# Expert rows turned by ScalarE and VectorE, hidden rows' transposes inside the gate/up product, and a second pair of PSUM banks for the down product

## The reference, cut to what matters

```python
h2 = rms_norm(x, norm2_g)
# each row picks the best of 4 groups, then 2 of the 8 experts in it (32 experts)
# its copies are sorted by expert and padded to blocks of 128 rows
def run_block(args):
    toks, e = args
    xb = h_pad[toks]                                         # 128 x 1024
    return (jax.nn.silu(xb @ w_gate[e]) * (xb @ w_up[e])) @ w_down[e]   # 256 hidden, 1024 out
ys = lax.map(run_block, ...) * slot_w
out = zeros.at[slot_tok].add(ys)                             # both experts of a row added
y = rms_norm(x + out, final_norm_g)
```

## Time and profile before

| | |
|---|---|
| three runs | 2896.26, 2897.02, 2900.2 us |
| profiled execution | the page gives its span alone, 2897.5 us |
| TensorE busy | 2851.8 us, 98% |
| VectorE, ScalarE, GpSimd busy | 54%, 28%, 30% |
| first stage | to about 1940 us |
| expert stage | from about 1960 us to the end, 80 blocks |
| mean over the span | 127 GB/s; 171 to 274 in most slices of the expert stage |

### The profile page before, as it was taken

How to read it: one execution, slowest core, us unless ns; L and a number is a source line. 1 busy time by engine, 2 the same in 40 slices (tenths; PEclk the granted TensorE clock), 3 DMA queues, 4 the chain that set the end, 5 groups by cost and what they waited for, 6 DMA issues and landing times.

```text
span 2897.5 us, 38361 instructions
## 1 busy us (share of the span) xinstructions
PE 2851.8 (98%) x12809; PEld 1883.5 (65%) x12809; DVE 1575.9 (54%) x4155; ACT 816.7 (28%) x1550; POOL 871.3 (30%) x1366
## 2 busy tenths in 40 slices
PE   8999999999999999999999999979999999999997
PEld 6776777777767767776777677744444444444443
DVE  5656565556555565556565656563444444444444
ACT  2223232322332232323232323222222222222222
POOL 1021111112111211121112111114656665665665
PEclk9999999999999999999999999989999999999999
DMA  7312121211122111211121211267675667567653
GB/s 308 141 52 72 60 74 52 73 70 63 52 73 76 56 59 66 81 52 59 66 81 52 73 59 66 75 224 266 235 267 186 227 202 253 200 222 274 237 171 124
DMA packets 109623, 369.01 MB, mean 127 GB/s; under 512 B 39497, under 2 KB 41426, under 8 KB 99442
## 3 DMA queue, kind: packets, MB, share of 16 engines
q1 hardware_dynamic: 48946, 252.91, 23.9%
q0 software_dynamic: 60480, 113.57, 11.9%
HBM read 325.09 MB, written 140.33 MB: 161 GB/s over the span
## 4 chain that ended last, share of the span: by engine, by line
PE 97%; DMA 1%; DVE 0%; issue 0%; ACT 0%; SPq 0%; POOL 0%; POOLq 0%; DVEq 0%; ACTq 0%
PE PB L368 24%; PE PB L1591 19%; PE PB L379 16%; PE PB L463 12%; PE SS L1631 9%; PE YB L463 4%; PE TB L1576 2%; PE YB L417 2%; PE TB L357 1%; DMA arena<-in_w_in 1%; PE SS L426 1%; PE TB L440 1%; PE SS L430 1%; PE TB L404 1%; PE YB L1624 1%; PE MB L408 1%
## 5 line engine op out<-in xcount | busy, mean ns | idle before, releaser
L368 PE MATMUL PB<-arena,hT 128*128 128x512 f32 (+2 forms) x2112 | 726.8, 497 | 1.7 <-DVE arena L1118 0.9
L368 PEld LDWEIGHTS PB<-arena,hT 128*128 128x128 f32 x2112 | 397.9, 191 | 270.5 <-issue 222.7
L1591 PE MATMUL PB<-arena,hT 128*128 x1296 | 569.3, 592 | 0.0
L379 PE MATMUL PB<-hT,arena 128*128 128x128 f32 x4224 | 487.2, 276 | 4.4 <-DVE arena L1106 4.4
L379 PEld LDWEIGHTS PB<-hT,arena 128*128 128x128 f32 x4224 | 481.8, 193 | 8.2 <-issue 4.6
L1591 PEld LDWEIGHTS PB<-arena,hT 128*128 128x128 f32 x1296 | 246.1, 190 | 309.8 <-issue 309.8
L1143 POOL TENSOR_SCALAR rs<-sq 128x2 f32<-128x2 f32 (+1 forms) x66 | 14.2, 215 | 1304.2 <-ACT h L735 958.0
L463 PE MATMUL PB<-arena,tT 128*128 128x274 f32 (+1 forms) x1056 | 357.8, 493 | 0.7 <-ACT tT L639 0.7
L1631 PE MATMUL SS<-arena,xdt 128*128 x640 | 287.9, 592 | 0.0
L463 PEld LDWEIGHTS PB<-arena,tT 128*128 128x128 f32 x1056 | 195.5, 190 | 140.8 <-issue 120.5
L808 DVE SCALAR_TENSOR_TENSOR xc<-xT,cols,xc 128x128 f32<-128x128 f32 x792 | 216.8, 347 | 3.5
(11 more groups left out here) (273 smaller groups left out, 3585.7 us busy)
## 6 DMA issues: line engine op xcount, KB each, us to landing
arena<-in_w_expert SPq DMA_DIRECT2D x32, 2048.0 KB
arena<-in_w_expert SPq DMA_DIRECT2D x32, 1024.0 KB
h_rows<-h SPq DMA_DIRECT2D x34, 512.0 KB, 2.7
x_in<-in_x_rows SPq DMA_DIRECT2D x33, 512.0 KB, 4.6
hT<-in_x_cols SPq DMA_DIRECT2D x33, 512.0 KB, 3.7
x_res<-in_x_rows SPq DMA_DIRECT2D x33, 512.0 KB, 5.1
dec<-running_sums SPq DMA_DIRECT2D x33, 512.0 KB, 3.7
first_rows<-bc SPq DMA_DIRECT2D x33, 512.0 KB, 3.9
```

What stands on the lines that cost most here:

```text
L368: mm = nc.tensor.matmul(out, hT[u][:, k, :], w_group(name)[:, k, :], start=k == 0, stop=k == KD - 1)
L379: mm = nc.tensor.matmul(PB[b][:, c * P:(c + 1) * P], w_block(name, c)[:, k, :], hT[u][:, k, :], start=k == 0, stop=k == KD - 1)
L1591: mm = nc.tensor.matmul(PB[u][:, :], hT[u][:, k, :], arena[:, bass.ds(slot + k * 2 * DE, 2 * DE)], start=k == 0, stop=k == KD - 1)
```

## The change

Three things change in the expert stage.

1. The rows of blocks 2 and on aren't transposed by TensorE. The 128 gathered rows are four quarters of 32. ScalarE copies three of them, in 12 copies of 32 partitions x 256 elements, so that 32x32 squares stand on the partitions where their turned form belongs (`moved`: `zz` and `btok`). VectorE turns 32x32 squares: the last quarter in four instructions straight from the gathered rows (`turn_last`), the moved quarters in two (`turn_moved`).
2. The hidden rows' two transposes stand after the fourth of the eight gate/up products of the next block.
3. The down product uses `SS` and `TB` in turn (`dn_bank`), so it waits for the evictions of the block two before.

With them the orders of work change on ScalarE, VectorE and GpSimd. Semaphores are merged (`smp_zero` into `smp_masks`, `lists_T` into `tab_rows`) to make room for two new ones.

```diff
@@ names used by all
+        moved = [zz[:, 0:DE], zz[:, DE:2 * DE], btok[:, :]]
+        def quarter(b, g, q):
+            return g_buf[b % GB][32 * g:32 * (g + 1), :].rearrange("p (c q i) -> p q c i", q=4, i=32)[:, q, :, :]
+        dn_bank = [[SS[:, n, :] for n in range(2)], [flat(TB[n]) for n in range(2)]]
@@ GpSimd
             def gather(b):
-                n = b % GB
-                after(pool, s["gx_T"], 2 * (b - GB + 1))
+                n, of = b % GB, b - GB
+                after(pool, s["gx_T"], 2 * (min(of, 1) + 1))
+                after(pool, s["rows_turned"], of - 1)
+            def keep(b):
+                for k in range(2):
+                    pool.wait_ge(s[f"dn_out{k}"], b + 1)
+                rows_to(first_d[:, :], y_buf[b % GB], first_i, b, first_kept)
             def step(b):
-                gather(b + AHEAD)
+                if b > 0:
+                    keep(b - 1)
+                residual(b)
+                gather(b + GB)
                 if b > 0:
                     pool.wait_ge(s["fin_sq"], b)
                     root_of(1 - b % 2, b)
-                for k in range(2):
-                    pool.wait_ge(s[f"dn_out{k}"], b + 1)
-                rows_to(first_d[:, :], y_buf[b % GB], first_i, b, first_kept)
-                residual(b + 1)
+                earlier(b)
                 if b > 0:
                     pool.wait_ge(s["fin_out"], b)
                     store(b - 1)
-                earlier(b + 1)
@@ TensorE
+        def pe_hidden(pe, b):   # the two transposes of line 1624, with their waits
+        def pe_down(pe, b, slot):
+            pe.wait_ge(s["hbT_out"], b + 1)
+            for n in range(2):
+                after(pe, s[f"dn_out{n}"], b - 1)
+                ...             # the four products, into dn_bank[b % 2][n]
             def step(b):
-                pe_gate_up(pe, b + 1)
-                ...             # the two transposes of line 1624
-                pe_rows(pe, b + 2)
-                ...             # the down product
+                weights = pe_weights(pe, b + 1)
+                slot = entry(pe, TAB_SLOT, b, 0, SLOT_AT[2])
+                pe_gate_up(pe, b + 1, weights, 0, 4)   # waits for rows_turned >= b and hb_ready >= b
+                pe_hidden(pe, b)
+                pe_gate_up(pe, b + 1, weights, 4, KD)
+                pe_down(pe, b, slot)
@@ ScalarE
+            def move(b, n0, n1):
+                if n0 == 0:
+                    act.wait_ge(gathered[b % GB], 16 * (b // GB + 1))
+                    after(act, s["rows_turned"], b - 2)
+                for n in range(n0, n1):
+                    g, q = n // 4, n % 4
+                    ins = nc.scalar.activation(moved[g][32 * q:32 * (q + 1), :], quarter(b, g, q), ACT.Copy)
+                if n1 == 12:
+                    ins.then_inc(s["rows_moved"], 1)
             def step(b):
-                ...             # hidden copy, silu(b + 1), rows0(b + 2), squares(b - 1, b), weigh
+                move(b + 2, 6, 12)
+                if b > 0:
+                    squares(b - 1, b)
+                hidden(b)
+                silu(b + 1)
+                move(b + 3, 0, 6)
+                weigh(b)
@@ VectorE
+            def turn_last(b):
+                dve.wait_ge(gathered[b % GB], 16 * (b // GB + 1))
+                dve.wait_ge(s["gu_full"], b)
+                for q in range(4):
+                    V.transpose(hT[b % 2][32 * q:32 * (q + 1), :, 96:128],
+                                quarter(b, 3, q))
+            def turn_moved(b):
+                dve.wait_ge(s["rows_moved"], b - 1)
+                V.transpose(hT[b % 2][:, :, 0:64].rearrange("p c (g t) -> p g c t", g=2),
+                            zz[:, :].rearrange("p (g c i) -> p g c i", g=2, i=32))
+                V.transpose(hT[b % 2][:, :, 64:96], btok[:, :].rearrange("p (c i) -> p c i", i=32)).then_inc(s["rows_turned"], 1)
             def step(b):
-                ...             # add_first(b - 1), gate(b + 1), rows1(b + 2), weigh, norm(b - 1), add x2
+                if b > 0:
+                    add_first(1 - b % 2, b, 16 * ((b + 1) // 2))
+                turn_moved(b + 2)
+                if b > 0:
+                    norm(1 - b % 2, b)
+                gate(b + 1)
+                turn_last(b + 3)
+                weigh(b)
+                add_x2(b)
```

More of the change, by code:

```diff
@@ L1580, in pe_weights, with pe_gate_up @@
             return entry(pe, TAB_SLOT, b, 0, SLOT_AT[2]), entry(pe, TAB_NTH, b, 1, NE) * 32
-        def pe_gate_up(pe, b, weights=None):
+        def pe_gate_up(pe, b, weights, k0, k1):
             u = b % 2
[L1585 to L1590, removed]
+            slot, loads = weights
+            if k0 == 0:
+                pe.wait_ge(w_loaded, loads)
+                if b < 2:
+                    for k in range(2):
+                        pe.wait_ge(s[f"gx_out{k}"], b + 1)
+                after(pe, s["rows_turned"], b - 1)
+                after(pe, s["hb_ready"], b - 1)
+            for k in range(k0, k1):
                 mm = nc.tensor.matmul(PB[u][:, :], hT[u][:, k, :], arena[:, bass.ds(slot + k * 2 * DE, 2 * DE)],
                                       start=k == 0, stop=k == KD - 1)
-            mm.then_inc(s["gu_full"], 1)
+            if k1 == KD:
+                mm.then_inc(s["gu_full"], 1)
+        def pe_hidden(pe, b):
+            pe.wait_ge(s["hb_ready"], b + 1)
+            after(pe, s["hbT_out"], b)
+            for k in range(2):
+                mm = nc.tensor.transpose(YBv[:, k, :], hb2[b % 2][:, k * P:(k + 1) * P], ident)
+            mm.then_inc(s["hbT_full"], 1)
+        def pe_down(pe, b, slot):
+            pe.wait_ge(s["hbT_out"], b + 1)
+            for n in range(2):
+                after(pe, s[f"dn_out{n}"], b - 1)
+                for k in range(2):
+                    mm = nc.tensor.matmul(dn_bank[b % 2][n], hTb[:, k, :],
+                                          arena[:, bass.ds(slot + KD * 2 * DE + k * D + n * 512, 512)], start=k == 0, stop=k == 1)
+            mm.then_inc(s["dn_full"], 1)
         def pe_table_rows(pe):
@@ L1617, in step @@
             def step(b):
-                u = b % 2
-                pe_gate_up(pe, b + 1)
+                weights = pe_weights(pe, b + 1)
                 slot = entry(pe, TAB_SLOT, b, 0, SLOT_AT[2])
[L1621 to L1625, removed]
-                pe_rows(pe, b + 2)
[L1627 to L1634, removed]
+                pe_gate_up(pe, b + 1, weights, 0, 4)
+                pe_hidden(pe, b)
+                pe_gate_up(pe, b + 1, weights, 4, KD)
+                pe_down(pe, b, slot)
             pe_rows(pe, 0)
             pe_rows(pe, 1)
-            pe_gate_up(pe, 0, weights0)
+            pe_gate_up(pe, 0, weights0, 0, KD)
             pe.wait_ge(s["smp_new"], 8)
@@ L1690, in gate, with add_first @@
                 V.tensor_tensor(hb2[u], silu_g[u], PB[u][:, DE:], ALU.mult).then_inc(s["hb_ready"], 1)
-            def add_first(u, back):
-                after(dve, first_back[u], back)
+            def add_first(u, n, back):
+                dve.wait_ge(s["x2_added"], n)
+                dve.wait_ge(first_back[u], back)
                 V.tensor_tensor(f_buf[u], f_buf[u], m_buf[u], ALU.add).then_inc(s["first_added"], 1)
@@ L1698, in norm, with weigh, add_x2 @@
                 V.scalar_tensor_tensor(out=f_buf[u], in0=f_buf[u], scalar=rs[:, u:u + 1], in1=gf_b, op0=ALU.mult, op1=ALU.mult).then_inc(s["fin_out"], 1)
-            def step(b):
-                u = b % 2
-                if b > 0:
-                    dve.wait_ge(s["x2_added"], b)
-                    add_first(1 - u, 16 * (b // 2))
-                gate(b + 1)
-                rows1(b + 2)
+            def weigh(b):
                 dve.wait_ge(s["dn_full"], b + 2)
                 after(dve, first_kept, 16 * (b - GB + 1))
-                V.tensor_scalar(y_buf[b % GB][:, 512:], SS[:, 1, :], wt[:, b:b + 1], None, ALU.mult).then_inc(s["dn_out1"], 1)
-                if b > 0:
-                    norm(1 - u, b)
+                V.tensor_scalar(y_buf[b % GB][:, 512:], dn_bank[b % 2][1], wt[:, b:b + 1], None, ALU.mult).then_inc(s["dn_out1"], 1)
+            def add_x2(b):
+                u = b % 2
                 for k in range(2):
```

56 lines of the change are left out of this document (25 added, 31 removed).

## The result

The change makes the kernel slower: 2959.1 us (median of 4, 2954.9 to 2969.6) against 2897.7, ratio 1.0218 (95%: 1.0198 to 1.0238). The forecast was 2854 us and a gain. The profiled execution took 2954.9 us, its span is 2953.1.

The account below looks back on a forecast made before the run. TensorE's instructions were taken as the bound of the expert stage, gapless at 11.39 us a block. The 2897.5 us span less 69.6 (row transposes) and 3.3 (ends) plus 29 (late gathers) gave 2854, range 2819 to 2886.

Parts of the forecast that it names:

- ends: First blocks and the tail after the last weighing: nothing gained at the start, last norm earlier, 3.3 us less.
- late earlier rows: waits of TensorE: Expert stage: late gathers of earlier rows stop TensorE through ScalarE's hidden-row copy; 0 to 55 us, about half taken, 29.
- rival B: The earlier-rows gather hides and TensorE runs gapless at 10.52 us a block: 2824.5 us, chance 0.24.
- What is taken from TensorE: Expert blocks: 80 x 0.87 us of row transposes go, about 70 us; hidden rows' transposes in mid product cost nothing.
- What ScalarE gets: Twelve small copies a block at 0.29 us, 3.5 us (upper end 4.6); ScalarE's block 5.8, at most 6.9 of 10.5.
- What VectorE gets: Turns of the rows, 2.8 us a block (2.3 to 5.6); VectorE's block 7.5, at the upper end 10.3.
- The waits: Loop through GpSimd and VectorE in the new orders: 10.0 us a block against 10.52, so it fits.
- the DMA whose cover shrinks: Gather of earlier rows: cover falls from 8.2 to 3.7 us, 2.1 more before TensorE stops; 29 us come back.
- Rival E: Something else, such as a lower granted clock after gaps or new instructions left on TensorE; chance 0.03.
- C: The GpSimd and VectorE loop, or the same 24 late gathers in full, takes most of the gain: 2875 us, chance 0.20.
- D: VectorE's turns are dear, over 0.77 us for 256 columns, making the kernel slower: 2921 us, chance 0.11.
- A: The forecast itself: earlier-rows gather collides with weight loads in part of the blocks, 2854 us (2838 to 2868), chance 0.42.

Follow-up runs that it names:

- no_earlier: The changed kernel without the gather of the earlier rows (first expert's part left out): 2826.9 us, ratio 0.9758 to the kernel before.
- late_hidden_end: Changed kernel with add_first, square, root, norm and store later, and the hidden rows' transposes back behind the whole gate/up product: 2897.7 us, 1.0001 to the kernel before.
- small_loads: The changed kernel with expert weight loads from the fourth slot use on cut to 64 columns each: 2827.2 us, ratio 0.9763 to the kernel before.
- copy_first: The changed kernel with ScalarE's copy of the hidden rows put ahead of the square: 2848.1 us, ratio 0.9831 to the kernel before.
- earlier_first: The changed kernel with the gather of the earlier rows ahead of the root on GpSimd: 2961.6 us, ratio 1.0215 to the kernel before.
- holds: The changed kernel without the earlier-rows gather, ScalarE held by idle copies ahead of the hidden rows' copy in 26 blocks: 2928.6 us, 1.0108 to the kernel before.

## Why the prediction was wrong

**Its sum, term by term.**

| term | forecast | measured |
|---|---|---|
| row transposes | -69.6 | -70 (0.87 to 0.88 x 80) |
| ends | -3.3 | 0 |
| start of the stage | none | -3 (it varies by 5 us between the kernels here) |
| late earlier rows: waits of TensorE | +29 (0 to 55) | +88.3 |
| clock and restart after these waits | none | +39.9 |

No_earlier stands for what is left when the last two terms are gone: 2825.2 us, where rival B had 2824.5. Adding 88.3 + 39.9 gives 2953.4; the span is 2953.1.

**What is taken from TensorE** held: 10.52 us a block, down product to gate/up without a gap. The down product is not slowed by transposes in mid product. The figure of the Trainium skill, left out of the sum, would have promised 176 us. What I did not see is that the mid-product place isn't a detail at no cost: without it the whole gain is gone (late_hidden_end). The 55 us that I had at nothing didn't enter the error, since the change has that place.

**What ScalarE gets** was under-sized: one copy 0.41 us, six in 2.53, so 0.42 from start to start, where I took 0.29 and had 0.38 as the upper end. The 0.28 of the earlier trace rows came from two instructions on 128 partitions that read PSUM; the copies here are of 32 partitions, from SBUF and strided, and no run tells which of these makes the difference. The Trainium skill, page "ScalarE: Activation LUTs", section "What ACT_TABLE_LOAD costs", gives 186 ns + 0.833 ns a column, less about 93 ns of overlap when they follow each other; an estimate from it is 0.31 us for 256 columns. Page and measurement differ, and the measurement decides: 0.42. It cost nothing, as ScalarE's 7.3 us a block (69.79 of 100 in no_earlier, times 10.52) still fit.

**What VectorE gets** held: 1.79 for four turns, 0.70 and 0.40, together 2.9 us (2.8 forecast); 7.6 us a block from the same window (7.5). The forecast took the dearer of two nearby rows, and the turns are about that dear.

**The waits** held in kind and in numbers: cover 3.7 us, slack of the copy 1.95 (2.1), the issue under norm 2.05 (2.04). The Trainium skill, page "SBUF — State Buffer", section "SBUF: two separate sides", tells of a port that VectorE and GpSimd share; the two lengths of an issue, 1.02 with VectorE free and 2.05 under its two-input operation, agree.

**The step that failed is "the DMA whose cover shrinks".** I said "between 0 and 55, I take about half, 29", as the request would follow an empty queue. The path was right, and so were the 15 to 30 blocks; its price wasn't, in three ways.
- The count should not have been halved. In the kernel before, 25 of 80 of these gathers took over 5.8 us from issue end to landing, 61.5 us in all beyond it. Afterwards 26 did, and TensorE waited 27 times. What GpSimd has in its queue is not the main reason for the delay; the weight load is (small_loads).
- The upper bound of 55 was no bound. It assumed that the lateness stays while all around it moves. It grew to 84 us beyond 5.8, and 88.3 is what TensorE waited. In copy_first it was 8. Why it grew is open.
- A wait of TensorE was priced at its length. Rival E had the clock and put it aside, "in A the gaps are short". Of 27 waits, 19 of 2.66 to 5.78 us cost mostly 1.7 to 2.0 each besides, two of them 2.9 and 3.2; the eight others, up to 2.21 us and one of 3.03, cost 0.26. Together 39.9 us.

The full 55 alone would have made 2880, and with 2 us for each of 24 waits 2928, slower than before: together the halving and the clock gave the forecast its sign.

**Ends.** The end of the span after, VectorE:

```profile
2937.74 0.75 DVE L1755 TENSOR_SCALAR wsT<-TB,bc 128x512 f32<-128x512 f32 x1
2938.58 1.22 DVE L1763 TENSOR_TENSOR arena<-wsT,bc 128x1024 f32<-128x1024 f32 x1
...
2941.92 1.23 DVE L1746 TENSOR_TENSOR arena<-arena,xT 128x1024 f32<-128x1024 f32 x1
...
2945.55 1.28 DVE L1750 SCALAR_TENSOR_TENSOR arena<-arena,rs 128x1024 f32<-128x1024 f32 x1 [2.40 <-POOL rs L1539]
```

From the end of the weighing to that of the last norm it takes 8.3 us; it was 9.5, and 6.3 were forecast. Between add_x2 and add_first 2.1 us go by with a copy, a loop's end and a memset, which I had as nothing. The weighing itself starts 0.7 us after TensorE's last product has ended, behind the last turns. From the end of that product to the end of the span it is 16.1 us before and after, so nothing was gained.

**The rivals.** B is what no_earlier and small_loads show. C's loop is real as a limit (earlier_first). D got only the sign, and not by its own cause: a turn of 256 costs 0.45, 0.32 below the 0.77 from which it decides. The true case is A's path at a price beyond its bounds, with the clock of E on top.

## What to carry to other kernels

When a change shortens the cover of a transfer, count in the trace how many of those transfers took longer than the new cover, with their whole landing times and not only their present waits, and take that sum without a discount. It is no bound: over 5.8 us it was 61.5 us before, and from 8 to 84 us in the kernels above. Price a wait of TensorE of some microseconds above its length. In an in-order queue, put what the bound engine needs ahead of what waits for a DMA: here a swap of two lines turned 2% slower into 1.7% faster.

## What the runs showed of the hardware

- After TensorE waits, the granted clock can fall to 1.2 GHz for 3.4 us, sometimes 6.8. In the kernel after and in holds waits up to 2.21 us cost 0.26 besides, those from 2.66 up mostly 1.7 to 2.0 and up to 3.2; but one of 3.03 and two of 3.83 cost 0.26. In earlier_first waits of 1.92 and 2.01 us already cost 1.96 each, with the clock at half, while one of 2.61 cost 0.26. So the length alone doesn't decide; what does isn't settled.
- The gather of the earlier rows (up to 128 rows of 4 KB, by the indirect queue) lands a median of 3.2 us after the end of its issue in the kernels before and after, and up to 11.2 beside weight loads; with the loads made small the median is 2.8 and the longest 6.8.
- ScalarE's copies of 32 partitions x 256 columns from SBUF start 0.42 us apart, a copy and a Silu of 128 x 256 from PSUM 0.28.
- VectorE turns float32 tiles of 256 columns in 0.40 to 0.45 us and 512 in 0.70. Eight transposes on TensorE take 0.87 to 0.88 in the stream, though each record says 0.27.
